# Cached values of a paged decode step: four pages per TensorE visit, and one value page loaded per slot

## The reference

```python
def moba_sample(q, k_new, v_new, cache_k, cache_v, page_table):
    ...
    gate = jnp.einsum('bqhd,bnhd->bhqn', qf, k_mean)      # 4 blocks of 2 pages
    _, sel = lax.top_k(gate, top)                         # 3 of the 4 blocks, per head
    ...
    p = jax.nn.softmax(jnp.concatenate([s for s, _, _ in parts], axis=-1), axis=-1)
    ...
        out = out + jnp.einsum('bhqk,bhqkd->bqhd', pb, vals.astype(jnp.float32))
```

## Time and profile before

| | |
|---|---|
| median of 3 runs | 469.51 us |
| span of the profiled execution | 467.2 us |
| what lies around the span, taken as median less span | 2.3 us |
| TensorE busy | 456.2 us, 98% |
| VectorE busy | 394.1 us, 84% |
| ScalarE busy | 294.4 us, 63% |
| GpSimd busy | 100.9 us, 22% |
| value products (L717) | 512 passes, 34.2 us |
| page loads | 64 of keys, 64 of values, 512 KB each |

### The profile page before, as it was taken

How to read it: one execution, slowest core, us unless ns; L and a number is a source line. 1 busy time by engine, 2 the same in 40 slices (tenths; PEclk the granted TensorE clock), 3 DMA queues, 4 the chain that set the end, 5 groups by cost and what they waited for, 6 DMA issues and landing times.

```text
span 467.2 us, 11345 instructions
## 1 busy us (share of the span) xinstructions
PE 456.2 (98%) x3855; PEld 413.8 (89%) x3855; DVE 394.1 (84%) x1610; ACT 294.4 (63%) x490; POOL 100.9 (22%) x181
## 2 busy tenths in 40 slices
PE   6999999999999999999999999999999999999997
PEld 4899899897879888888899889899898898899997
DVE  3898899699999799999899999799999774668861
ACT  4966545686984496995486695666948357324430
POOL 2040421013323213423321332321223110000000
PEclk9999999999999999999999999999999999999999
DMA  8899699749999999999999999998999985457511
GB/s 304 322 353 407 183 322 371 240 158 340 317 416 408 404 368 354 412 410 408 408 380 315 409 412 409 411 372 303 382 415 409 410 334 188 149 180 261 182 48 48
DMA packets 44858, 150.91 MB, mean 323 GB/s; under 512 B 6192, under 2 KB 7796, under 8 KB 44672
## 3 DMA queue, kind: packets, MB, share of 16 engines
q1 hardware_dynamic: 20368, 70.77, 40.8%
q0 software_dynamic: 19008, 67.20, 37.3%
q10 hardware_dynamic: 5424, 12.21, 6.8%
HBM read 137.37 MB, written 12.76 MB: 321 GB/s over the span
## 4 chain that ended last, share of the span: by engine, by line
PE 70%; ACT 10%; DVE 10%; DMA 4%; issue 4%; ACTq 1%; POOLq 0%; SPq 0%; POOL 0%; DVEq 0%
PE pj L534 28%; PE pj L537 13%; PE wk L534 6%; PE pa L717 4%; PE wk L537 3%; DMA kpages<-in_cache_k 3%; DVE kpages L1170 3%; DVE wlo L1071 2%; ACT L838 2%; ACT whi L818 2%; PE wk L487 2%; DVE cslot L1252 2%; PE wk L639 2%; PE wk L673 1%; DMA cst<-in_consts 1%
## 5 line engine op out<-in xcount | busy, mean ns | idle before, releaser
L534 PE MATMUL pj<-xn,whi 128*128 128x264 f32 x1328 | 180.8, 288 | 1.6 <-ACT mqT L976 1.3
L534 PEld LDWEIGHTS pj<-xn,whi 128*128 128x128 f32 x1328 | 168.4, 189 | 10.2 <-issue 6.2
L1071 DVE TENSOR_TENSOR wlo<-wraw,whi 128x1024 fp32r<-128x1024 f32 x112 | 136.1, 1220 | 8.8 <-ACT whi L818 8.3
L818 ACT ACTIVATE whi<-wraw 128x1024 fp32r<-128x1024 f32 x112 | 117.9, 1053 | 23.1 <-PE wk L537 12.9
L1170 DVE CUSTOM_DVE_ANT_0 kpages<-kpages,qbc 128x128 f32<-128x128 f32 x512 | 115.5, 292 | 5.3 <-DMA kpages<-in_cache_k 5.1
L537 PE MATMUL pj<-xn,wlo 128*128 128x264 f32 x664 | 93.8, 284 | 0.4 <-DVE wlo L1071 0.4
L537 PEld LDWEIGHTS pj<-xn,wlo 128*128 128x128 f32 x664 | 85.5, 188 | 0.6 <-DVE wlo L1071 0.6
L404 POOL DMA_DIRECT2D kpages<-in_cache_k x64 | 34.3, 536 | 165.9 <-DVE sco L1170 141.9
L404 POOL DMA_DIRECT2D vpages<-in_cache_v x64 | 33.9, 530 | 57.9 <-issue 38.9
L1170 DVE DVE_READ_ACCUMULATOR2_ANT sco<- 128x1 f32 x512 | 42.8, 84 | 0.0
L717 PE MATMUL pa<-vpages,prob 128*32 128x256 f32 x512 | 34.2, 385 | 1.7 <-ACT prob L876 1.7
(11 more groups left out here) (271 smaller groups left out, 615.0 us busy)
## 6 DMA issues: line engine op xcount, KB each, us to landing
wraw<-in_weights SPq DMA_DIRECT2D x112, 512.0 KB, 6.8
kpages<-in_cache_k POOLq DMA_DIRECT2D x64, 512.0 KB, 8.1
vpages<-in_cache_v POOLq DMA_DIRECT2D x64, 512.0 KB, 10.8
cslot<-in_states SPq DMA_DIRECT2D x16, 512.0 KB, 9.4
out_C_s<-cslot ACTq DMA_DIRECT2D x16, 512.0 KB, 8.1
xres<-in_tokens SPq DMA_DIRECT2D x1, 1056.0 KB, 5.5
out_k_p<-kT ACTq DMA_DIRECT2D x4, 256.0 KB, 10.2
out_v_p<-v_nat ACTq DMA_DIRECT2D x4, 256.0 KB, 4.7
```

What stands on the lines that cost most here:

```text
L534: mm(bank[:, 0:T], whi[:, q, k, :], src[:, g, k, :], start=(k == 0 and g == 0), stop=False)
L818: A(whi[:, n % WSPLIT], wraw[:, n % WRAW], ACT.Copy).then_inc(whi_ready, 1)
L1071: V.tensor_tensor(wlo[:, n % WRAW], wraw[:, n % WRAW], whi[:, n % WSPLIT], ALU.subtract).then_inc(wlo_ready, 1)
```

## The change

`value_quad` takes the place of `value_pair`: a visit now takes four pages, at lags 13 and 17, so a sample has two visits instead of four. `value_load` issues one value page of the next sample per slot, at lags 14 to 21, instead of two pages in every second slot at lags 13 to 19. The number of products, of waits before a page and of loads stays.

```diff
+VISIT = 4
 ...
-def value_pair(g):
-
-    for p in range(PAGES // 2):
-        b = due(g, VALUES + 2 * p)
+def value_quad(g):
+
+    for p in range(PAGES // VISIT):
+        b = due(g, VALUES + VISIT * p)
         if b is not None:
             return b, p
+    return None
+
+
+def value_load(g):
+
+    for p in range(PAGES):
+        b = due(g, VALUES + 1 + p)
+        if b is not None and b + 1 < NB:
+            return (b + 1) * PAGES + p
     return None
 ...
-                pair = value_pair(g)
-                if pair is not None:
-                    for s in range(pair[0] * PAGES + 2 * pair[1] + VSLOTS, pair[0] * PAGES + 2 * pair[1] + VSLOTS + 2):
-                        if s < NB * PAGES:
-                            values(s)
+                if value_load(g) is not None:
+                    values(value_load(g))
 ...
-                    for pg in (2 * pair[1], 2 * pair[1] + 1):
+                    for pg in range(VISIT * quad[1], VISIT * (quad[1] + 1)):
```

More of the change, by code:

```diff
@@ L705, in cache_side @@
                     mm(page_sums[b % 2], ones, sco[:, b % 2].rearrange("p a h -> p (a h)"), start=True, stop=True).then_inc(g_ps, 1)
[L706 to L709, removed]
+                quad = value_quad(g)
+                if quad is not None:
+                    b = quad[0]
+                    if quad[1] == 0:
                         pe.wait_ge(prob_ready, b + 1)
                         pe.wait_ge(accr_ready, b)
-                    for pg in (2 * pair[1], 2 * pair[1] + 1):
+                    for pg in range(VISIT * quad[1], VISIT * (quad[1] + 1)):
                         s = b * PAGES + pg
```

## The result

The kernel after takes 474.63 us (median of 4 runs, 473.82 to 476.78), the kernel before 469.48 beside it: ratio 1.0117, 95% interval 1.0095 to 1.0138. The forecast was 468.5.

The account below looks back on a forecast made before the run. TensorE, busy 456.2 of 467.2 us, was taken as the main bound, with stretches set by ScalarE and VectorE. Chain walk -1.2, late pages +0.5, sum -0.7, taken as -1.0: 469.5 to 468.5 us, range 465.3 to 471.8.

Parts of the forecast that it names:

- A visit's cost on TensorE: On TensorE, a four-page visit costs 2.07 us against 2.40 for two two-page visits; 16 removed visits save 5.3 us.
- How much reaches the end: Walk along the chain: doubled visits add 0.87 us, removed ones save 1.20, many lost in waits; about -1.2 us at the end.
- The pure rival: TensorE decides nearly everywhere and all 5.3 us pass: 464.2 to 467.1 us, most likely 466; chance 0.28.
- TensorE's idle time grows at the exponentials: Sign at samples 4 and 6: TensorE idles more; its 0.22 us wait at 354.12 would be near 2.
- The forecast's last step: At the sum, a little of what ScalarE and the key pages may give takes -0.7 to -1.0 us.
- The number of GpSimd's issues is the same, and nothing is added to its queue: GpSimd's load queue: 64 issues of each, 0.53 to 0.55 us each, off the chain; no gain counted, up to 1 us kept for the range.
- Late value pages: At samples 2, 4 and 6, TensorE may wait up to 3.6 us each for the last page; 0.2 average, 0.5 in all.
- The lead that I had worked out: Time from issue to need for the last value pages: 12.5 us at sample 4, 12.1 at sample 6.
- My argument that the shorter queue would help: The queue holds fewer value pages at samples 2, 4 and 6, so page waits were taken as 0.2 us on average.
- The key pages: VectorE's two waits for late key pages, 5.1 us, bound what less GpSimd waiting is worth; no gain counted, up to 1 us for the range.
- late value pages, say 473: Slower rival: last pages of samples 2, 4 and 6 arrive late, three waits of 2 to 3.6 us; +2.5 to +9; chance 0.16.
- The sign that I had named for it: In the timeline, waits for value pages of over 2 us would show the second rival, late value pages.

Follow-up runs that it names:

- The visits alone: The kernel before with four-page visits, its value pages still loaded in pairs, two in every second slot: 468.80 us, ratio 0.9993 to the kernel before.
- the fifth experiment: The kernel after with the decay rows' loads issued ahead of their slot's value page and every value page loaded one slot earlier: 468.00 us, ratio 0.9967 to before.
- The loads alone: The kernel after with two-page visits as before, keeping one value page loaded per slot: 471.64 us, ratio 1.0045 to the kernel before.
- loads a slot earlier: The kernel after with each value page loaded one slot earlier: 471.66 us, ratio 1.0049 to the kernel before.
- rows and spread first: Four-page visits with paired loads as before, with loading and spreading of the decay rows moved ahead of the value pages: 472.34 us, ratio 1.0063 to before.
- rows ahead of the page: The kernel after with the decay rows' loads issued ahead of the value page of their slot: 472.79 us, ratio 1.0083 to the kernel before.
- one visit of eight pages: The kernel after with one eight-page visit a sample, decay rows on ScalarE's queue, two value pages in each of slots 13 to 16: 477.71 us, ratio 1.0163.
- eighth: Four-page visits with value pages loaded as before, decay rows loaded by ScalarE's queue: 468.38 us, ratio 0.9981 to the kernel before.
- ninth experiments: The kernel after with decay rows loaded by ScalarE's queue and every value page one slot earlier: 467.33 us, ratio 0.9951 to the kernel before.
- rows on the other queue: The kernel before with only the decay rows' two loads moved to ScalarE's queue: 469.26 us, ratio 1.0000 to the kernel before.

## Why the prediction was wrong

- **A visit's cost on TensorE (0.33 us saved for each removed): right.** 32 passes take 1.87 us, 16 times. TensorE's busy time falls by 3.9 to 4.4 us in the profiles of four-page visits without the lower clock (451.8 to 452.3), somewhat less than 5.3.
- **How much reaches the end (-1.2 us): right in size.** The visits alone end 0.5 us earlier, which is not clear of noise. With the rows and the pages out of the way the kernel after gains 2.0 (467.33 against 469.33). The pure rival, that all 5.3 us pass, has no run for it. As predicted, TensorE's idle time grows at the exponentials: with both remedies (the fifth experiment) it waits 1.53 us at 276.07, where it waited 0.74 in the kernel before, and 0.71 at 354.30 instead of 0.22; I had put the second near 2. The forecast's last step, from -0.7 to -1.0, had no row behind it.
- **"The number of GpSimd's issues is the same, and nothing is added to its queue ... GpSimd is not on the chain": this is the step that failed.** The count was right and the conclusion wrong. An issue that is moved changes what stands ahead of its neighbours, and slot 13 had a neighbour with a consumer: the rows. I had followed only the key pages and the value pages through the queue. VectorE paid for it with more than the 2.7 us that it was ahead at this place (I had looked at another, where it was 0.5), and TensorE behind it. The loads alone lose 2.4 us by this.
- **Late value pages (0.2 on average, 0.5 in all): the mechanism was right, the size was not.** The lead that I had worked out, 12.1 us, came out as 11.7 (362.60 to 374.26, the start of the visit plus 1.5), and the page took 12.8. One slot of lead more is worth 2.97 us in the kernel after, and about 4.8 where the rows are ahead (472.79 to 468.00, on two chips). My argument that the shorter queue would help failed: the pages took 11.8 and 12.8 us, not much less than the 13.0 of the earlier trace rows, which was the median of four pages.
- **What a wait costs: not in the prediction.** The lower clock behind a wait took 1.7 us in the profile after. How much of the median it is stays open: of its four runs three have a mean clock of 0.996 (473.82, 475.20, 476.78), one has 1.000 (474.06) and is no faster than the fastest of the others.
- **The key pages: right.** VectorE's wait of 5.1 us for them fell to 0.2, ScalarE's 2.2 went, and no run shows that either was worth anything at the end. GpSimd's wait for the visits fell only from 19.1 to 10.2; I had written near nothing.
- **The rival "late value pages, say 473"** came near the time with half of the cause. The runs do not credit it with the whole: with no late page left (loads a slot earlier) the kernel is still slower than before by 0.49%. The sign that I had named for it, waits of over 2 us for a page, does not stand in the profile after, where the longest is 1.21.

## What to carry to other kernels

When loads are moved in a queue, list every instruction of that queue in the slots touched, small ones above all, with what now stands ahead of it, who waits for it and how far ahead that engine is; an unchanged number of issues says nothing. When work on a buffer is gathered into a bigger piece, the last part of it is needed earlier and its successor can be loaded only later, so the load has to move forward, not back. And two delays can cover one another: taking one away alone (1.8 or 3.0 us here) can undervalue the pair (6.6), so run the combination before judging either.

## What the runs showed of the hardware

- **A 1 KB load was about as slow as a page.** In the kernel after, the two rows that GpSimd issued at 261.41 and 261.91 landed after 8.0 and 9.1 us, the 512 KB value page just ahead of them after 9.4, at 418 GB/s on all queues together. It was not the page of the same slot alone: with the visits alone, where none stood ahead of them, the two rows landed after 7.8 and 10.1 us, in the kernel before after 7.2 and 7.9. The Trainium skill (DMA: Bandwidth & Descriptors, Anatomy of one DMA) has about 2.0 us plus the bytes at 436 GB/s; by it a row would take an estimated 2.0 us. Here pages are in flight beside the rows, and the measurement decides.
- **The clock behind a wait.** It fell to the lower level, for some 3 us, behind TensorE's waits of 1.75 us at 276.68 (kernel after), 1.81 at 275.88 (loads a slot earlier) and 2.06 at 275.20 (rows and spread first); it did not behind the 2.32 us at 373.42 (rows ahead of the page), nor behind 1.92 and 2.10 with one visit of eight pages. What tells these apart stays open. Of the 33 runs of the fifth, eighth and ninth experiments, whose TensorE has no wait above 1.6 us behind the first 20 us of the profile, none had a mean clock below 0.999. But with the kernel before and its rows on the other queue, where the longest such wait is 0.75, one run of 12 has 0.996 (472.40 us). That the lower clock accounts for the scatter of some kernels is read from their clocks alone, and two kernels do not bear it out; no run held TensorE busy through a wait to test it.
